# Attention values as the stationary operand, one-pass mask with minimum head by head, and normalized probabilities, in one layer of a hybrid GLA and windowed-attention backbone

## The chip, the cores and the metric

One core of a Trainium2 chip runs the whole kernel. The metric is device time in microseconds (us), from start to end of one execution. All figures below come from the measured times or from one profiled execution of the kernel before.

## The reference, cut to what matters

One layer on 512 latent tokens (four tiles of 128) and 128 context tokens (a fifth tile), D_MODEL 2048. The change touches only the windowed attention: 16 query heads of width 64 in four groups of four, each group sharing one key and value head. A latent tile reads its own and its neighbour key blocks, plus the cached context block; the context tile reads itself alone.

```
def sink_softmax(score_list, sink):
    s_sink = sink.astype(jnp.float32).reshape(SWA_KV_HEADS, SWA_GROUP, 1, 1)
    m = s_sink
    for sc in score_list:
        m = jnp.maximum(m, jnp.max(sc, axis=-1, keepdims=True))
    ps = [jnp.exp(sc - m) for sc in score_list]
    den = jnp.exp(s_sink - m)
    for p in ps:
        den = den + jnp.sum(p, axis=-1, keepdims=True)
    return [p / den for p in ps]
...
    p_ctx, p_band = sink_softmax([s_ctx, s_band], sink)
    o = jnp.einsum('bnhgqk,bkhd->bnqhgd', p_ctx, cvf) + jnp.einsum('bnhgqk,bnkhd->bnqhgd', p_band, vw)
```

Around it: modulated norm, one input projection (its last chunks are the queries), the gated linear attention, then two branch products with sigmoid gates ("the gate products"), an output product, a second norm, a router and 16 experts.

## The kernel before, in words

Every engine has its own instruction stream, written out by hand; semaphores join them. Large products run in "pieces" of 128 rows of weights: ScalarE rounds a piece's weights and tokens (the high halves, L458 and L459), VectorE subtracts them from the originals (the low halves, L462 and L465), TensorE makes three products for each token tile (L837). Four buffers of pieces (`spW`, `spX`) lie in memory that the attention stage uses for its own buffers. In the gate products VectorE also adds up a row of modulation for most pieces (L387, L390, in `mod_sums`).

The attention stage stands between the query projection and the gate products. It has 20 units: `units` orders them as tile 0 to 4 for key heads 0 and 1, then tile 0 to 4 for key heads 2 and 3, so that units 0 and 1 are tile 0, units 2 and 3 tile 1, and so on, and again from unit 10. A unit is four query heads of one tile against 3, 4, 4, 3 or 1 key blocks of 128 for tiles 0 to 4. Its steps:

- `scores(u)` on TensorE (L1110): four heads, each into its own PSUM bank (0 to 3). It waits for `sc_m`, the masks of the whole unit before, and signals `sc_pe` once.
- `softmax_front(u)` on VectorE: for each head one fused instruction scales, adds the mask and takes the maximum (L1932), then two small operations give the sink's difference and the negated maximum (L1938, L1939).
- `softmax_exps(u)` on ScalarE (L1544, L1547): waits for all of that, then the sink's exponential and four exponentials with their sums.
- `p_transposes(i)` on TensorE (L1138): four transposes of key block i into bank 4 or 5. Blocks 0 and 2 are copied out by ScalarE (L1564), blocks 1 and 3 by VectorE (L1956).
- `values(i)` on TensorE (L1148): for each of four heads one matmul, the transposed probabilities 128x128 stationary and 64 columns of values moving, output token by head width in bank 6.
- `o_rows(u)` on VectorE (L1963) multiplies by one over the sum; `o_transposes(u)` on TensorE (L1122) turns the result in bank 7, and `copy_o(u)` on ScalarE (L1553) puts it into `swT`, in the iteration after.
- `softmax_sums(u)` on VectorE (L1945, L1946): sum with the sink and reciprocal.

The loop over u issues, on TensorE: scores(u+2), transposes 0 and 1, then alternately a transpose and a value block; on ScalarE: copies of blocks 0 and 2 of u, copy_o(u-1), exponentials of u+2; on VectorE: copy of block 1, sums of u, masks of heads 0 and 1 of u+2, copy of block 3, masks of heads 2 and 3, o_rows(u). In the first four iterations VectorE also applies the rotary embedding to one of four remaining query tiles (`rope_q`, three operations of 512 columns), after a permutation on TensorE (`q_permuted`, L1079). Behind the loop ScalarE and VectorE prepare pieces 0 to 2 of the gate products, and those products begin.

## Time and profile before

| | |
|---|---|
| device time, median of 3 runs | 3020.17 us (3017.7 to 3020.69) |
| profiled execution | 3019.33 us, its span 3017.1 us, mean granted clock 0.978 |
| TensorE matmul busy | 2866.1 us (95% of the span) |
| VectorE busy | 2060.9 us (68%) |
| ScalarE busy | 1598.1 us (53%) |
| attention stage | 738.4 to 886.2 us from the span's start |

A share of busy time is an average over stages with different limits. What the change is worth is read from the attention stage alone: from the first score product (738.39) to the first matmul of the gate products (886.23). A matmul's record holds its latency too, and consecutive matmuls overlap, so their pace is read from the distance between starts.

### The profile page before, as it was taken

What the parts mean: (1) busy time and instruction counts of PE and PEld (TensorE: products, weight loads), DVE (VectorE), ACT (ScalarE), POOL (GpSimd) and SP (SyncE); (2) the same over time, 40 slices, a digit from 0 to 9 for tenths busy, and PEclk for the clock granted to TensorE, in tenths of its full rate; (3) what the DMA queues carried; (4) which work ended last, traced back from release to release, by engine and by line L of the source; (5) the groups of instructions that cost most, each with busy time, mean ns of one, the idle gap of its engine ahead of it and who ended that gap; (6) DMA issues with size and microseconds to landing.
All of it is one profiled execution on the core that took longest, in us unless ns stands there. A gap on an engine that the chain in (4) does not pass through costs nothing.

```text
span 3017.1 us, 38938 instructions
## 1 busy us (share of the span) xinstructions
PE 2866.1 (95%) x14261; PEld 2145.1 (71%) x14261; DVE 2060.9 (68%) x2367; ACT 1598.1 (53%) x1919; POOL 281.5 (9%) x182
## 2 busy tenths in 40 slices
PE   6999889999989999999999987999999999999993
PEld 4798548898878888887888873666666666666662
DVE  2436664544666667767665555888888888888884
ACT  4245324443554444434433343777777777777773
POOL 0000010000000000000001001111112112211111
PEclk9999999999999999999999997999999999999996
DMA  9822342221014343343462269999999999999994
GB/s 372 285 70 70 131 167 73 84 65 57 1 31 135 116 156 127 113 147 123 143 244 89 70 235 367 401 404 392 387 390 378 382 387 389 384 383 390 387 389 170
DMA packets 160799, 685.04 MB, mean 227 GB/s; under 512 B 13940, under 2 KB 14020, under 8 KB 99004
## 3 DMA queue, kind: packets, MB, share of 16 engines
q1 hardware_dynamic: 147216, 613.45, 53.2%
q0 software_dynamic: 11408, 69.78, 7.3%
q8 instruction: 78, 1.28, 0.2%
q10 hardware_dynamic: 2064, 0.26, 0.1%
q14 instruction: 33, 0.27, 0.0%
HBM read 651.91 MB, written 31.60 MB: 227 GB/s over the span
## 4 chain that ended last, share of the span: by engine, by line
PE 91%; DVE 4%; ACT 2%; DMA 2%; issue 1%; POOL 0%; DVEq 0%; POOLq 0%; ACTq 0%; SPq 0%
PE ps L837 38%; PE ps L1312 23%; PE ps L1339 12%; PE ps L856 5%; PE ps L863 3%; PE ps L1148 1%; PE ps L1285 1%; PE ps L1110 1%; PE ps L801 1%; DMA ring<-w_mod 1%; PE ps L1138 1%; ACT ar L1547 1%; PE ps L1006 1%; PE ps L1249 1%; PE ps L971 1%
## 5 line engine op out<-in xcount | busy, mean ns | idle before, releaser
L837 PE MATMUL ps<-split_weights,split_tokens 128*128 128x512 f32 x5040 | 1159.3, 391 | 8.1 <-issue 3.8
L837 PEld LDWEIGHTS ps<-split_weights,split_tokens 128*128 128x128 f32 x5040 | 944.8, 188 | 216.6 <-issue 16.7
L1312 PE MATMUL ps<-split_experts,split_xsT 128*80 128x512 f32 x3072 | 709.7, 392 | 4.8 <-DVE split_experts L2097 4.8
L1312 PEld LDWEIGHTS ps<-split_experts,split_xsT 128*80 128x80 f32 x3072 | 455.1, 148 | 257.6 <-DVE split_experts L2097 5.8
L462 DVE TENSOR_TENSOR split_weights<-ring,split_weights 128x512 fp32r<-128x512 f32 x384 | 267.8, 697 | 536.7 <-ACT split_tokens L459 534.8
L458 ACT ACTIVATE split_weights<-ring 128x512 fp32r<-128x512 f32 x384 | 242.7, 632 | 734.8 <-PE ps L837 612.3
L2097 DVE TENSOR_TENSOR split_experts<-hT,split_experts 128x2048 fp32r<-128x2048 f32 x240 | 548.0, 2289 | 77.2 <-ACT split_experts L1659 77.1
L1659 ACT ACTIVATE split_experts<-hT 128x2048 fp32r<-128x2048 f32 x240 | 460.7, 1920 | 153.6 <-PE ps L1312 114.4
L1339 PE MATMUL ps<-split_experts,split_hidT 128*80 128x512 f32 x1536 | 361.0, 394 | 0.0
L1339 PEld LDWEIGHTS ps<-split_experts,split_hidT 128*80 128x80 f32 x1536 | 225.5, 148 | 121.9
L465 DVE TENSOR_TENSOR split_tokens<-hT,split_tokens 128x640 fp32r<-128x640 f32 x304 | 249.4, 820 | 0.0
L2097 DVE TENSOR_TENSOR split_experts<-ring,split_experts 128x2048 fp32r<-128x2048 f32 x96 | 218.5, 2289 | 22.5 <-ACT split_experts L1659 22.5
L459 ACT ACTIVATE split_tokens<-hT 128x640 fp32r<-128x640 f32 x304 | 219.8, 723 | 0.0
L1659 ACT ACTIVATE split_experts<-ring 128x2048 fp32r<-128x2048 f32 x96 | 184.0, 1917 | 60.8 <-PE ps L1312 33.9
L856 PE MATMUL ps<-split_tokens,split_weights 128*128 128x384 f32 x768 | 185.8, 351 | 9.2 <-DVE split_tokens L489 9.2
L390 DVE SCALAR_TENSOR_TENSOR cst<-ring,cond,cst 128x512 f32<-128x512 f32 x240 | 169.1, 746 | 0.0
L856 PEld LDWEIGHTS ps<-split_tokens,split_weights 128*128 128x128 f32 x768 | 129.0, 194 | 24.1 <-DVE split_tokens L489 12.6
L863 PE MATMUL ps<-split_tokens,split_weights 128*128 128x256 f32 x768 | 136.5, 288 | 3.0 <-ACT ar L1520 1.8
L737 POOL DMA_INDIRECT y_rows<-ar,sidx x16 | 108.3, 6766 | 267.4 <-DVE ar L2125 267.4
L2097 DVE TENSOR_TENSOR split_experts<-ar,split_experts 128x2048 fp32r<-128x2048 f32 x48 | 109.7, 2286 | 28.6 <-ACT split_experts L1659 28.6
L863 PEld LDWEIGHTS ps<-split_tokens,split_weights 128*128 128x128 f32 x768 | 126.3, 193 | 4.0 <-ACT ar L1520 2.1
L1659 ACT ACTIVATE split_experts<-ar 128x2048 fp32r<-128x2048 f32 x48 | 91.9, 1915 | 21.5 <-PE ps L1312 13.0
(264 smaller groups left out, 1997.3 us busy)
## 6 DMA issues: line engine op xcount, KB each, us to landing
ring<-w_mod SPq DMA_DIRECT2D x96, 1024.0 KB, 5.3
hT<-w_exp_gate SPq DMA_DIRECT2D x80, 1024.0 KB, 7.2
hT<-w_exp_up SPq DMA_DIRECT2D x80, 1024.0 KB, 7.1
hT<-w_exp_down SPq DMA_DIRECT2D x80, 1024.0 KB, 9.3
ring<-w_in SPq DMA_DIRECT2D x64, 1024.0 KB, 5.3
ring<-w_exp_gate SPq DMA_DIRECT2D x32, 1024.0 KB, 8.0
ring<-w_exp_up SPq DMA_DIRECT2D x32, 1024.0 KB, 10.2
ring<-w_exp_down SPq DMA_DIRECT2D x32, 1024.0 KB, 7.5
```

The costliest lines, as they stand in the source:

```text
L390: dve.scalar_tensor_tensor(acc, v, c, acc, ALU.mult, ALU.add).then_inc(z_rd, 1)
L458: self.eng.activation(spW[:, s, 0, :], raw, ACT.Copy)
L459: self.eng.activation(spX[:, s, 0, :], (src[k] if type(src) is dict else src[:, k, :]), ACT.Copy).then_inc(piece_high, 1)
L462: a = self.eng.tensor_tensor(spW[:, s, 1, :], raw, spW[:, s, 0, :].bitcast(F32), ALU.subtract)
L465: self.eng.tensor_tensor(spX[:, s, 1, :], (src[k] if type(src) is dict else src[:, k, :]), spX[:, s, 0, :].bitcast(F32), ALU.subtract).the ...
L837: mm = pe.matmul(ps[:, b, :], spX[:, s, x, b * P:(b + 1) * P], spW[:, s, w, :], start=(k == 0 and x == w), stop=(k == n_k - 1 and x == 1))
L856: mm = pe.matmul(ps[:, c, 0:TA], spW[:, s, w, c * P:(c + 1) * P], spX[:, s, x, 0:TA], start=(k == 0 and x == w), stop=(k == KT - 1 and w = ...
L863: mm = pe.matmul(ps[:, 4 + c // 2, (c % 2) * TB:(c % 2 + 1) * TB], spW[:, s, w, c * P:(c + 1) * P], spX[:, s, x, TA:TOK], start=(k == 0 an ...
L1312: mm = pe.matmul(ps[0:CAP, bank + i, :], xsT[:, x, k, :], spE[:, s, w, col:col + BANK], start=(k == 0 and x == w), stop=(k == KT - 1 and x ...
L1339: mm = pe.matmul(ps[0:CAP, 4 + n, :], hidT[:, x, k, :], spE[:, s, w, n * BANK:(n + 1) * BANK], start=(k == 0 and x == w), stop=(k == FT - ...
L1659: act.activation(spE[:, s, 0, :], exp_slot[j % ESLOTS], ACT.Copy).then_inc(piece_high, 1)
L2097: dve.tensor_tensor(spE[:, s, 1, :], exp_slot[j % ESLOTS], spE[:, s, 0, :].bitcast(F32), ALU.subtract)\
```

## The change

The values become the stationary operand: two matmuls for each key block instead of four, each with 64 columns of values stationary and 256 columns of transposed probabilities (two heads) moving. Their output is already transposed, so that `o_rows`, `o_transposes` and their buffer go, and `copy_o(u)` reads bank 6 in the same iteration. The division by the sum moves ahead of the transposes: four multiplications of the probabilities in memory for each unit (`softmax_back`). The fused mask operation works on negated scores with a minimum, so that the negation of the maximum goes; it signals for each head, and scores and exponentials wait head by head. VectorE copies block 1 alone, between the masks of head 1 and head 2 of unit u+2; ScalarE copies blocks 0, 2 and 3. `q_permuted` stands ahead of the value products. The last two units have buffers of their own, and pieces 0 to 2 of the gate products are prepared during them.

```
-        orow = area(26112, 2, GRP * HD)
+        last_S = [area(27264 + BANK * i, BANK) for i in range(2)]
+        last_pT = [area(26112 + BANK * i, BANK) for i in range(2)]
-        copied_by = [(pt_cd if i % 2 else pt_cp) for t, _ in units for i, _ in enumerate(unit_keys(t)[1])]
+        n_units = len(units)
+        def S_of(u):
+
+            if u >= n_units - 2:
+                return last_S[u % 2].rearrange("p (j n) -> p j n", j=GRP)
+            return Sbuf[u % 3].rearrange("p (j n) -> p j n", j=GRP)
+
+        def pT_of(u, i):
+            return last_pT[u % 2] if u >= n_units - 2 else pT[:, u % 2, i * BANK:(i + 1) * BANK]
+
+        copied_by = [(pt_cd if i == 1 else pt_cp) for t, _ in units for i, _ in enumerate(unit_keys(t)[1])]
+        def copy_pT(act, u):
+
+            for i, _ in enumerate(unit_keys(units[u][0])[1]):
+                if i != 1:
+                    n = first_block[u] + i
+                    act.wait_ge(pt_pe, n + 1)
+                    if 2 <= u < n_units - 2:
+                        act.wait_ge(pv_pe, u - 1)
+                    act.activation(pT_of(u, i), ps[:, 4 + n % 2, :], ACT.Copy).then_inc(pt_cp, 1)
+
+        def copy_o(act, u):
+            t, g = units[u]
+            act.wait_ge(pv_pe, u + 1)
+            act.activation(swT[:, 2 * g:2 * g + 2, t * P:(t + 1) * P],
+                           ps[:, 6, 0:2 * P].rearrange("p (c q) -> p c q", c=2), ACT.Copy).then_inc(pv_cp, 1)
@@ -1099,28 +1124,18 @@
             def scores(u):
                 t, g = units[u]
-                if u:
-                    pe.wait_ge(sc_m, u)
                 for j in range(GRP):
+                    if u:
+                        pe.wait_ge(sc_mx, (u - 1) * (GRP + 1) + j + 1)
-                mm.then_inc(sc_pe, 1)
-
-            def o_transposes(u):
-
-                pe.wait_ge(pv_cp, u + 1)
-                pe.wait_ge(sq_rp, min(4 + u + 1, 8))
-                if u:
-                    pe.wait_ge(k_cp, 2 * SKV + u)
-                for c in range(2):
-                    mm = pe.transpose(ps[:, 7, c * P:(c + 1) * P], orow[:, u % 2, c * P:(c + 1) * P], ident)
-                mm.then_inc(k_tr, 1)
+                    mm.then_inc(sc_pe, 1)
@@ -1131,12 +1146,12 @@
-                        pe.wait_ge(sc_e, u + 1)
+                        pe.wait_ge(sc_n, u + 1)
-                                          Sbuf[u % 3][:, j * BANK + i * P:j * BANK + (i + 1) * P], ident)
+                                          S_of(u)[:, j, i * P:(i + 1) * P], ident)
-                    for j in range(GRP):
-                        mm = pe.matmul(ps[:, 6, j * HD:(j + 1) * HD],
-                                       pT[:, u % 2, i * BANK + j * P:i * BANK + (j + 1) * P],
-                                       svr[:, blocks[i], g * HD:(g + 1) * HD],
+                    for half in range(2):
+                        lo = half * HD
+                        mm = pe.matmul(ps[lo:lo + HD, 6, 0:2 * P], svr[:, blocks[i], g * HD:(g + 1) * HD],
+                                       pT_of(u, i).rearrange(
+                                           "p (c e q) -> p c e q", c=2, e=2)[:, :, half, :],
                                        start=(i == 0), stop=(i == len(blocks) - 1), skip_group_check=True)
+                if u < 4:
+                    q_permuted(4 + u)
+                else:
+                    if u == 4:
+                        pe.wait_ge(sq_rp, 8)
                 for i in range(len(blocks)):
                     if i + 2 < len(blocks):
                         p_transposes(i + 2)
                     values(i)
-                    if i == 0 and u:
-                        o_transposes(u - 1)
-                if u < 4:
-                    if u:
-                        pe.wait_ge(k_cp, 2 * SKV + u)
-                    q_permuted(4 + u)
-
-            o_transposes(len(units) - 1)
-            pe.wait_ge(k_cp, 2 * SKV + len(units))
+
+            pe.wait_ge(pv_cp, len(units))
             def softmax_exps(u):
-                act.wait_ge(sc_mx, u + 1)
                 sf = soft[:, u % 2]
-                act.activation(sf[:, 3, :], sf[:, 3, :], ACT.Exp)
                 for j in range(GRP):
-                    s = Sbuf[u % 3][:, j * BANK:j * BANK + len(blocks) * P]
-                    a = act.activation(s, s, ACT.Exp, bias=sf[:, 1, j:j + 1], accum_out=sf[:, 2, j:j + 1])
-                a.then_inc(sc_e, 1)
-
-            def copy_o(u):
-                t, g = units[u]
-                act.wait_ge(k_tr, SKV + u + 1)
-                act.activation(swT[:, 2 * g:2 * g + 2, t * P:(t + 1) * P],
-                               ps[:, 7, 0:2 * P].rearrange("p (c q) -> p c q", c=2), ACT.Copy).then_inc(k_cp, 1)
+                    act.wait_ge(sc_mx, u * (GRP + 1) + j + 1)
+                    s = S_of(u)[:, j, 0:len(blocks) * P]
+                    act.activation(s, s, ACT.Exp, bias=sf[:, 0, j:j + 1], scale=-1.0, accum_out=sf[:, 2, j:j + 1])
+                act.wait_ge(sc_mx, (u + 1) * (GRP + 1))
+                act.activation(sf[:, 3, :], sf[:, 3, :], ACT.Exp).then_inc(sc_e, 1)
 
             softmax_exps(0)
             softmax_exps(1)
             for u in range(len(units)):
-                for i in range(0, len(unit_keys(units[u][0])[1]), 2):
-                    act.wait_ge(pt_pe, first_block[u] + i + 1)
-                    if u >= 2:
-                        act.wait_ge(pv_pe, u - 1)
-                    to, src = pT_place(u, i)
-                    act.activation(to, src, ACT.Copy).then_inc(pt_cp, 1)
-                if u:
-                    copy_o(u - 1)
+                if u == n_units - 2:
+                    act.wait_ge(pv_pe, n_units - 2)
+                    gate_split(sp, 0, 0, 0, 1)
+                if u == n_units - 1:
+                    gate_split(sp, 0, 0, 1, AHEAD)
+                copy_pT(act, u)
                 if u + 2 < len(units):
                     softmax_exps(u + 2)
-            copy_o(len(units) - 1)
+                copy_o(act, u)
-            gate_split(sp, 0, 0, 0, AHEAD)
-            def softmax_front(u, heads):
-                dve.wait_ge(sc_pe, u + 1)
-                if u >= 3:
+                if 3 <= u < n_units - 2:
                 lo = {0: C_SW + P, 3: C_SW3, 4: C_SW + P}.get(t, C_SW)
                 for j in heads:
-                    a = dve.tensor_tensor_reduce(S[:, j, :], ps[:, j, 0:nk], cst[:, lo:lo + nk], HD ** -0.5,
-                                                 sink[:, GRP * g + j:GRP * g + j + 1], ALU.add, ALU.max,
-                                                 sf[:, 0, j:j + 1])
-                if GRP - 1 in heads:
-                    a.then_inc(sc_m, 1)
-                    dve.wait_ge(sc_m, u + 1)
-                    dve.tensor_tensor(sf[:, 3, :], sink[:, GRP * g:GRP * g + GRP], sf[:, 0, :], ALU.subtract)
-                    dve.tensor_scalar(sf[:, 1, :], sf[:, 0, :], -1.0, None, ALU.mult).then_inc(sc_mx, 1)
-
-            def softmax_sums(u):
-
+                    dve.wait_ge(sc_pe, u * GRP + j + 1)
+                    dve.tensor_tensor_reduce(S_of(u)[:, j, 0:nk], ps[:, j, 0:nk], cst[:, lo:lo + nk], -HD ** -0.5,
+                                             sink[:, GRP * g + j:GRP * g + j + 1], ALU.add, ALU.min,
+                                             sf[:, 0, j:j + 1]).then_inc(sc_mx, 1)
+                if GRP - 1 not in heads:
+                    return
+                dve.wait_ge(sc_mx, u * (GRP + 1) + GRP)
+                dve.tensor_tensor(sf[:, 3, :], sf[:, 0, :], sink[:, GRP * g:GRP * g + GRP], ALU.subtract).then_inc(sc_mx, 1)
+
+            def softmax_back(u):
                 sf = soft[:, u % 2]
                 dve.wait_ge(sc_e, u + 1)
                 ch.step(dve.tensor_tensor(sf[:, 2, :], sf[:, 2, :], sf[:, 3, :], ALU.add))
                 ch.step(dve.reciprocal(sf[:, 4, :], sf[:, 2, :]))
-
-            def copy_pT(u, i):
-
...
-            def o_rows(u):
-
-                dve.wait_ge(pv_pe, u + 1)
-                if u >= 2:
-                    dve.wait_ge(k_tr, SKV + u - 1)
-                dve.tensor_tensor(orow[:, u % 2, :].rearrange("p (j d) -> p j d", j=GRP),
-                                  ps[:, 6, 0:2 * P].rearrange("p (j d) -> p j d", j=GRP),
-                                  soft[:, u % 2, 4, :].unsqueeze(2).to_broadcast([P, GRP, HD]), ALU.mult).then_inc(pv_cp, 1)
-            softmax_front(0, range(GRP))
-            softmax_front(1, range(GRP))
+                for j in range(GRP):
+                    s = S_of(u)[:, j, 0:nk]
+                    a = dve.tensor_scalar(s, s, sf[:, 4, j:j + 1], None, ALU.mult)
+                a.then_inc(sc_n, 1)
+
+            ch.step(dve.tensor_scalar(sink[:, :], sink[:, :], -1.0, None, ALU.mult))
+            softmax_front(0)
+            softmax_front(1)
             for u in range(len(units)):
-                copy_pT(u, 1)
-                softmax_sums(u)
+                softmax_back(u)
                 if u + 2 < len(units):
                     softmax_front(u + 2, range(0, 2))
-                copy_pT(u, 3)
+                if len(unit_keys(units[u][0])[1]) > 1:
+                    n = first_block[u] + 1
+                    dve.wait_ge(pt_pe, n + 1)
+                    if u >= 2:
+                        dve.wait_ge(pv_pe, u - 1)
+                    dve.tensor_copy(pT_of(u, 1), ps[:, 4 + n % 2, :]).then_inc(pt_cd, 1)
                 if u + 2 < len(units):
                     softmax_front(u + 2, range(2, GRP))
-                o_rows(u)
                 if u < 4:
                     rope_q(4 + u)
-
+                if u == n_units - 2:
+                    dve.memset(mod_ones, 1.0).then_inc(z_rd, 1)
+                    gate_split(sp, 0, 0, 0, 1)
+
+            gate_split(sp, 0, 0, 1, AHEAD)
```

## Rows read from the trace of the kernel before

**Rows 1.** Busy time by stretch: us, then busy us (instructions) by engine, PEclk, DMA share

```profile
738.40:784.90 46.50, 40.90 (x295) 33.76 (x295) 31.49 (x90) 24.07 (x65) 0.00 (x0) 0.89 0.00 1
784.90:877.10 92.20, 84.42 (x735) 77.08 (x735) 53.88 (x201) 53.97 (x166) 0.00 (x0) 1.00 0.01 1
877.10:886.20 9.10, 3.83 (x30) 2.97 (x29) 3.34 (x11) 5.49 (x15) 1.17 (x1) 0.99 0.10 16
2000.00:2200.00 200.00, 200.00 (x912) 131.35 (x911) 175.56 (x95) 150.14 (x95) 38.23 (x12) 1.00 0.99 388
```

**Rows 2.** Timeline of TensorE, one iteration (u = 13): start us, us, what

```profile
841.67 2.11 PE L1110 MATMUL ps<-ar 64*128 64x384 f32 x16
843.70 1.09 PE L1138 MATMUL ps<-cst,ar 128*128 128x128 f32 x8
845.05 0.66 PE L1138 MATMUL ps<-cst,ar 128*128 128x128 f32 x4 [0.25 <-ACT ar L1564]
845.54 1.00 PE L1148 MATMUL ps<-ar 128*128 128x64 f32 x8
846.38 0.39 PE L1122 MATMUL ps<-cst,ar 128*128 128x128 f32 x2
846.60 0.60 PE L1138 MATMUL ps<-cst,ar 128*128 128x128 f32 x4
847.04 2.79 PE L1148 MATMUL ps<-ar 128*128 128x64 f32 x24
849.76 1.68 PE L1110 MATMUL ps<-ar 64*128 64x256 f32 x16
```

**Rows 3.** Timeline of TensorE in the linear attention, 64 stationary and 256 moving columns

```profile
405.21 1.95 PE L1006 MATMUL ps<-ar 128*64 128x256 f32 x16
...
418.64 0.65 PE L1006 MATMUL ps<-ar 128*64 128x256 f32 x4
```

**Rows 4.** Groups of VectorE by form, 600 to 900 us: busy us, mean ns | idle

```profile
L1932 DVE CUSTOM_DVE_ANT_0 ar<-ps,cst,sink 128x512 f32<-128x512 f32 x32 | 22.4, 747 | 0.3
L1932 DVE CUSTOM_DVE_ANT_0 ar<-ps,cst,sink 128x384 f32<-128x384 f32 x32 | 18.1, 615 | 19.3 <-PE ps L1110 19.1
L1956 DVE COPY ar<-ps 128x512 f32<-128x512 f32 x24 | 16.6, 692 | 34.2 <-PE ps L1138 34.2
...
L387 DVE TENSOR_SCALAR cst<-ring,cond 128x512 f32<-128x512 f32 x2 | 0.9, 482 | 0.0
```

**Rows 5.** Groups of ScalarE by form, 600 to 900 us

```profile
L1564 ACT ACTIVATE ar<-ps 128x512 f32<-128x512 f32 x36 | 21.3, 592 | 19.5 <-PE ps L1138 19.1
...
L1553 ACT ACTIVATE ar<-ps 128x256 f32<-128x256 f32 x20 | 7.7, 384 | 13.5 <-PE ps L1122 13.5
```

**Rows 6.** Chain that ended last: start us, us; four heads' exponentials, 512 and 128 columns

```profile
757.59 2.82 ACT ar L1547 x8
...
875.97 1.64 ACT ar L1547 x8
```

**Rows 7.** Timeline of the stage's start: first scores, second scores, third, first transposes

```profile
738.39 1.68 PE L1110 MATMUL ps<-ar 64*128 64x256 f32 x16 [1.14 <-ACT ar L1537]
742.40 2.88 PE L1110 MATMUL ps<-ar 64*128 64x256 f32 x16 [2.33 <-DVE soft L1932]
747.61 3.95 PE L1110 MATMUL ps<-ar 64*128 64x384 f32 x16 [2.33 <-DVE soft L1932]
751.49 2.46 PE L1138 MATMUL ps<-cst,ar 128*128 128x128 f32 x12
```

**Rows 8.** Busy time and granted clock (PEclk) by microsecond, the stretches at half clock

```profile
743.00:744.00 1.00, 1.00 (x9) 0.93 (x8) 0.00 (x0) 1.00 (x5) 0.00 (x0) 0.50 0.05 16
...
888.00:889.00 1.00, 1.00 (x4) 0.74 (x3) 1.00 (x3) 0.06 (x1) 0.00 (x0) 0.50 0.00 0
```

**Rows 9.** Timeline of a unit of tile 3 and of the stage's end, all engines

```profile
804.66 0.71 PE L1110 MATMUL ps<-ar 64*128 64x128 f32 x8
...
875.14 1.90 PE L1148 MATMUL ps<-ar 128*128 128x64 f32 x16
...
883.37 0.62 ACT L458 ACTIVATE split_weights<-ring 128x512 fp32r<-128x512 f32 x1
...
884.52 0.62 ACT L458 ACTIVATE split_weights<-ring 128x512 fp32r<-128x512 f32 x1
...
885.26 0.82 DVE L465 TENSOR_TENSOR split_tokens<-hT,split_tokens 128x640 fp32r<-128x640 f32 x1
...
886.23 14.00 PE L837 MATMUL ps<-split_weights,split_tokens 128*128 128x512 f32 x54 [3.17 <-DVE split_tokens L465]
```

More of the change, by code:

```diff
@@ L340, in build @@
         sq_pm, sq_rp, kv_ld = sem("rope_permuted"), sem("roped"), sem("cache_loaded")
-        k_dup, k_tr, k_cp, k_pm, k_rp, kv_st = (sem("k_doubled"), sem("k_then_o_transposed"), sem("k_then_o_copied"),
+        k_dup, k_tr, k_cp, k_pm, k_rp, kv_st = (sem("k_doubled"), sem("k_transposed"), sem("k_copied"),
                                                 sem("k_permuted"), sem("k_roped"), sem("cache_stored"))
-        sc_pe, sc_m, sc_mx, sc_e, pt_cd = sem("scores"), sem("scores_masked"), sem("scores_max"), sem("probs_exp"), sem("pT_copied_by_vector")
-        pt_pe, pt_cp, pv_pe, pv_cp = sem("p_transposed"), sem("pT_copied"), sem("pv_product"), sem("o_rows_normalized")
+        sc_pe, sc_mx, sc_e, sc_n, pt_cd = sem("scores"), sem("scores_masked_and_max"), sem("probs_exp"), sem("probs"), sem("pT_copied_by_vector")
+        pt_pe, pt_cp, pv_pe, pv_cp = sem("p_transposed"), sem("pT_copied"), sem("pv_product"), sem("pv_copied")
         gt_pe, gt_act, gt_dve = sem("gate_products"), sem("gate_sigmoid"), sem("gate_merged")
@@ L416, in build @@
         first_block = [sum(len(unit_keys(units[v][0])[1]) for v in range(u)) for u in range(len(units) + 1)]
-        copied_by = [(pt_cd if i % 2 else pt_cp) for t, _ in units for i, _ in enumerate(unit_keys(t)[1])]
+        n_units = len(units)
[6 more added lines that the diff above has]
+        copied_by = [(pt_cd if i == 1 else pt_cp) for t, _ in units for i, _ in enumerate(unit_keys(t)[1])]
         def pT_copied(pe, n):
             pe.wait_ge(copied_by[n], sum(c is copied_by[n] for c in copied_by[:n + 1]))
-        def pT_place(u, i):
-            return pT[:, u % 2, i * BANK:(i + 1) * BANK], ps[:, 4 + (first_block[u] + i) % 2, :]
+        def copy_pT(act, u):
[11 more added lines that the diff above has]
+                           ps[:, 6, 0:2 * P].rearrange("p (c q) -> p c q", c=2), ACT.Copy).then_inc(pv_cp, 1)
         def parts(*places):
@@ L1918, in _, with softmax_front @@
                     rope_q((k - 7) // 2)
-            def softmax_front(u, heads):
+            def softmax_front(u, heads=range(GRP)):
                 t, g = units[u]
-                _, blocks = unit_keys(t)
-                nk = len(blocks) * P
-                S = Sbuf[u % 3].rearrange("p (j n) -> p j n", j=GRP)[:, :, 0:nk]
+                nk = len(unit_keys(t)[1]) * P
                 sf = soft[:, u % 2]
-                dve.wait_ge(sc_pe, u + 1)
-                if u >= 3:
+                if 3 <= u < n_units - 2:
                     dve.wait_ge(pt_pe, first_block[u - 2])
@@ L1931, in softmax_front @@
                 for j in heads:
-                    a = dve.tensor_tensor_reduce(S[:, j, :], ps[:, j, 0:nk], cst[:, lo:lo + nk], HD ** -0.5,
-                                                 sink[:, GRP * g + j:GRP * g + j + 1], ALU.add, ALU.max,
-                                                 sf[:, 0, j:j + 1])
-                if GRP - 1 in heads:
-                    a.then_inc(sc_m, 1)
-                    dve.wait_ge(sc_m, u + 1)
-                    dve.tensor_tensor(sf[:, 3, :], sink[:, GRP * g:GRP * g + GRP], sf[:, 0, :], ALU.subtract)
-                    dve.tensor_scalar(sf[:, 1, :], sf[:, 0, :], -1.0, None, ALU.mult).then_inc(sc_mx, 1)
-            def softmax_sums(u):
+                    dve.wait_ge(sc_pe, u * GRP + j + 1)
[7 more added lines that the diff above has]
+            def softmax_back(u):
+                t, g = units[u]
+                nk = len(unit_keys(t)[1]) * P
                 sf = soft[:, u % 2]
@@ L2003, in gates_dve @@
                     dve.tensor_tensor(mrow[:, b, :], mrow[:, b, :], mtmp[b], ALU.add).then_inc(gt_dve, 1)
-            dve.wait_ge(pv_pe, len(units))
-            dve.memset(mod_ones, 1.0).then_inc(z_rd, 1)
-            gate_split(sp, 0, 0, 0, AHEAD)
             with dve.Fori(0, 3) as n:
```

7 lines of the change are left out of this document (removed).

## The prediction

> **What bounds the kernel now.** I read the 40 slices of the page first, then the busy time by stretch, then the timeline of TensorE through the attention stage, then the waits and the chain there. Outside the stage nothing is edited except the place of three pieces' preparation, so only the stage counts. It falls into three stretches [rows 1]: 46.5 us from the first score product to the first transposes of unit 4, 92.2 us to the last value product of unit 17, 9.1 us to the first gate product; 147.8 us together. In the middle one TensorE is busy 84.4 of 92.2 us at full clock (2.4 GHz), VectorE and ScalarE 54 each: TensorE bounds it, and its own order fixes the length. One iteration shows how [rows 2]: from 841.67 scores take 2.03, transposes 0 and 1 and the wait for ScalarE's copy of block 0 take 1.35, transpose 2 0.49, value block 0 0.84, the output's transposes 0.22, transpose 3 0.44, three value blocks 2.72; 8.09 us. The start is different: scores, masks and scores take turns, so that TensorE idles 2.33 us twice [rows 7], and the granted clock then falls to 0.50, its 1.2 GHz level [rows 8]; scores that take 2.11 us later take 3.95 there [rows 2, 7].
>
> **Part 1, the value products.** Removed are four matmuls for each block (0.84 us, or 0.9 in the run of three) and two output transposes (0.22 us) for each unit [rows 2]. Added are two matmuls with 64 columns stationary and 256 moving, each two records. The linear attention runs this very shape, also alternating between output partitions 0 and 64: 16 records in 1.95 us with the last one's latency, 4 in 0.65 [rows 3]. So four records, a block, cost 0.47 to 0.65; I take 0.50, nearer to the long run, since the next block follows at once. Four blocks save about 1.5 us, plus 0.22.
> The same rows speak on a rule. Sixteen records of 256 columns in 1.95 us [rows 3] are 0.46 to 0.48 ns a column; the sixteen score records of 384 and 128 columns in 2.03 us [rows 2] are 0.50. The pace of a column is the same, so the two halves do not overlap here. The Trainium skill ("TensorE: Matmul & The Clock Gate", in the section on why this matters for your kernels) says that matmuls with few output columns in distinct column groups run concurrently. By that rule a block would cost about half; its result is a rival below.
>
> **Part 2, VectorE.** Removed for each unit: the negated maximum, the second copy and the row multiplication. Added: four multiplications of the probabilities. The nearest row is a multiplication by a per-partition scalar of 512 columns from memory to memory, 482 ns [rows 4], against 692 for the copy from PSUM of the same size [rows 4]; two of them take 0.9 us together, and consecutive VectorE records overlap by some 0.08, so the pace is 0.41 for 512 columns. From 615 to 747 ns for 384 and 512 columns of the mask [rows 4], a block of 128 costs 0.13 at full rate, so about 0.07 here at the rate that 482 suggests: 0.34 for 384, 0.2 for 128. Bounds: 0.41 and 0.65 (the copy's pace). One iteration of four blocks on VectorE is then: masks 4 x 0.67 = 2.7, small operations 0.2, one copy 0.65, sums and reciprocal 0.4, multiplications 1.65; 5.6 us, in the shadow of TensorE as long as TensorE needs more. Once at the stage's start sixteen sinks are negated while the last projection still runs: nothing, and 0.2 us if it did not.
>
> **Part 3, ScalarE.** It gains the copy of block 3 (592 ns), keeps copy_o (384 ns) [rows 5] and the exponentials: four heads take 2.82 us for 512 columns and 1.64 for 128 [rows 6], so 2.43 for 384; the sink's adds 0.2. copy_o(u) now stands behind the exponentials of u+2, and ahead of copy 0 of u+1. Behind this queue stands transpose 2 of the next unit on TensorE, and value block 0 waits for copy_o itself since bank 6 is one. An iteration of four blocks on ScalarE from the start of copy 0: 0.6, wait for transpose 2 0.75, copies 2 and 3 1.35 with the wait between, exponentials 3.05, copy_o 0.4: 6.15 us. That is almost TensorE's own time, and where it is more, TensorE waits.
>
> **Part 4, the start and the first four iterations.** Scores and exponentials now follow each mask. Times from 738.39: first mask at 0.5, eight masks of 384 columns at 0.54 (615 ns less the overlap) and small operations to 5.2; scores(1) and scores(2) run in between, head by head. Sums and multiplications of unit 0: 0.4 + 4 x 0.34, so first transposes at 7.0; before, at 13.1 [rows 7]. Then VectorE bounds, since the rotary embedding stands in its queue: each of the four iterations has four masks of 512 (2.9 with the small ones), a copy 0.65, three operations of 512 columns for the embedding (2.15 at the copy's 692 ns), and the sums and multiplications of u+1 (1.75 once, 2.05 three times). 4 x 5.7 + 1.75 + 6.15 = 30.7. TensorE needs 2.0 + 1.2 + 0.9 (the permutation, which now fills the wait for copy 0) + about 2.6, less than 7.6. Unit 4's transposes start at 7.0 + 30.7 = 37.7, before at 46.5: 8.8 us gained.
>
> **Part 5, the middle.** From the first transpose of a unit to its last value product: 1.3 to transpose 2, 0.5 for it, 0.5 for value block 0, 0.44 for transpose 3, 3 x 0.48; 4.2 us for four blocks (six units: 25.2), 3.3 for three blocks (six units: 19.8), 1.8 and 2.0 for the two units of one block. Scores between them: 2.03 four times for four blocks [rows 2], 1.61 five times for three blocks (units 7, 10, 11, 16 and 17; 1.68 less the overlap) [rows 2], and 0.65 four times for one [rows 9]; 18.8 us. ScalarE's lateness, gone through unit by unit with Part 3's times: 1.05 for unit 6 and 1.1 for unit 16 (a short score product follows long exponentials), 0.55 for unit 14, and 0.1 to 0.2 five times; 3.45 us. Sum: 25.2 + 19.8 + 3.8 + 18.8 + 3.45 = 71.0 us against 92.2: 21.2 gained. VectorE finishes each unit's multiplications about 0.8 us before TensorE asks.
>
> **Part 6, the end.** Pieces 0 to 2 do not start before the last units, they start inside them and in ScalarE's queue: piece 0 waits for the values of unit 17 and stands ahead of unit 18's copy; pieces 1 and 2 stand ahead of unit 19's copy. A piece takes ScalarE 1.15 us (883.37 to 884.52) [rows 9]. From unit 17's last value: 1.2 + copy 0.65 + value 0.6 + copy_o 0.45 + two pieces 2.4 + copy 0.65 + value 0.6 + copy_o 0.45 + start 0.1 = 7.1 us, against 9.1 [rows 1]: 2.0 gained. VectorE's low halves and sums for piece 0 stand ahead of unit 19's multiplications, about 2.3 us, and end before ScalarE's pieces do. The preparation that stood exposed behind the stage (883.37 to 886.08) is covered by the two copies' waits only in part.
>
> **Sum.** Stage 37.7 + 71.0 + 7.1 = 115.8 against 147.8: 32 us. The profiled execution takes 3019.3 us (span 3017.1 and 2.2 around it), so 2987.3; it lies 0.8 under the median of 3020.17, which gives 2988. One cost has no row: three more waits for each score product. Its lower bound is zero, or a little less since they let scores start earlier; the upper is 0.1 us each, about 5 us in all. A satisfied wait between value blocks shows no gap in [rows 2], so I take it near zero, 1 us, and say 2989.
>
> **The rivals.**
> 1. VectorE bounds everywhere: if the multiplications run at 0.65, an iteration of four blocks takes 6.5 there, 0.2 above TensorE's, and each of the first four 0.9 longer: 5 us less gained, 2994. Against it speak 482 ns [rows 4].
> 2. The value products cost more: a strided moving operand could halve the rate, which gives 0.86 a block, as before. Then 50 blocks x 0.36 less what ScalarE's wait already holds, some 15 us less: 3004. No row has this stride; the shape itself is at full rate [rows 3].
> 3. The halves overlap: a block at 0.25. TensorE gets faster than ScalarE's 6.15, so only about 4 us come of it: 2985. [rows 3] speak against.
> 4. The gain is given back later. The experts run at a DMA share of 0.99 with 388 GB/s, and TensorE at 200 of 200 us [rows 1]. If the loads were bound to a time of their own, 3020 would stay. Against it: each load waits for a slot that TensorE and VectorE release, and the share before the experts is far lower (the page's slices), so the loads move with the rest.
> 5. Slower: the clock. With work cut by a fifth while VectorE and ScalarE set the pace, TensorE's idle parts could bring its clock down to 1.2 GHz again and again, as two idle times of 2.33 us did [rows 7, 8]. At that level an iteration of four blocks holds 5.8 us of work twice, about 12 us instead of 6.3. From six such iterations on (31 / 5.7) the gain is gone; with ten it ends at 2989 + 57 = 3046. Against it: the 7.8 idle us of the middle, in pieces, left the clock at 1.00 [rows 1], and the new pieces are by Part 5 mostly below 1.1 us.
>
> **How the numbers follow.** The forecast as worked out, with its unknowns, 2982 to 2998: 0.62. Rival 1: 0.09. Rival 2 in whole or part: 0.10. Rival 3: 0.08. Rival 4: 0.05. Rival 5: 0.06, of which a third ends still faster than before. The range of 2981 to 3003 holds the first, rivals 1 and 3 and a part of 2. 0.2% (6 us) is about what a measurement of this kernel can tell from no change. Faster by more: 0.91; within: 0.05; slower: 0.04.
>
> **What would show it.** First transposes of unit 0 near 7 us behind the first scores, and no score product of 2.9 or 3.95 us; value records four to a block at a pace of 0.12; multiplications at 0.48 for 512 columns; an iteration of four blocks at 6.2 to 6.4, TensorE idle before transpose 2 on ScalarE; last value of unit 17 at about 847, gate products at about 854. The prediction falls if the clock is at 0.50 in the middle, if value records stand 0.2 apart, or if TensorE waits for the multiplications in every unit.

## The result and the profile after

The changed kernel takes 2984.51 us (median of four, 2983.78 to 2985.76) against 3019.37 (median of four): ratio 0.9885, 95% interval 0.9868 to 0.9902, 34.9 us. The forecast was 2989, in a range of 2981 to 3003. The profiled execution took 2985.76 us, its span 2983.9, against 3019.33 and 3017.1.

The attention stage goes from 738.39 to 886.23 before, 147.8 us, and from 738.49 to 856.81 after, 118.3 us: 29.5 us. The two spans differ by 33.2 us; of the rest, 3.8 us lie behind the stage, where nothing is edited, and the repetition ("Changed again") returns to them. Busy time by stretch after, cut as [rows 1] is (us, then busy us and instructions of TensorE, its weight loads, VectorE, ScalarE, GpSimd; granted clock; DMA share; GB/s):

```profile
738.50:776.00 37.50, 32.16 (x232) 22.89 (x232) 35.60 (x101) 25.00 (x69) 0.00 (x0) 1.00 0.00 1
776.00:847.60 71.60, 65.82 (x528) 45.40 (x528) 61.92 (x221) 54.44 (x167) 0.00 (x0) 1.00 0.01 1
847.60:856.80 9.20, 3.55 (x16) 1.69 (x16) 7.22 (x19) 6.39 (x17) 0.16 (x1) 0.74 0.00 0
```

46.5, 92.2 and 9.1 us [rows 1] have become 37.5, 71.6 and 9.2. VectorE is busy 35.6 of the first 37.5 us: it bounds there. TensorE is busy 65.8 of the 71.6 us of the middle. The end has gained nothing, and its granted clock is 0.74 where it was 0.99.

The start, timeline of all engines (start us, us, what, idle before and who ended it), to be held against [rows 7]:

```profile
738.49 6.85 PE L1135 MATMUL ps<-ar 64*128 64x256 f32 x48 [1.14 <-ACT ar L1551]
739.56 0.62 DVE L1935 CUSTOM_DVE_ANT_0 ar<-ps,cst,sink 128x384 f32<-128x384 f32 x1 [13.55 <-PE ps L1135]
...
740.22 0.61 ACT L1560 ACTIVATE ar<-ar,soft 128x384 f32<-128x384 f32 x1 [0.49 <-DVE soft L1935]
...
744.67 1.41 DVE L1953 TENSOR_SCALAR ar<-ar,soft 128x384 f32<-128x384 f32 x4
...
746.13 1.09 PE L1153 MATMUL ps<-cst,ar 128*128 128x128 f32 x8 [0.80 <-DVE ar L1953]
```

The three score products run as one stretch beside the masks, the exponentials follow the first mask by 0.66 us, and the first transposes come 7.64 us behind the first scores instead of 13.1. The clock stays at 1.00 through the whole first stretch.

The same iteration as [rows 2] (u = 13), TensorE after:

```profile
820.03 2.11 PE L1135 MATMUL ps<-ar 64*128 64x384 f32 x16
822.06 1.09 PE L1153 MATMUL ps<-cst,ar 128*128 128x128 f32 x8
823.41 0.66 PE L1153 MATMUL ps<-cst,ar 128*128 128x128 f32 x4 [0.25 <-ACT ar L443]
823.99 0.65 PE L1164 MATMUL ps<-ar 128*64 128x256 f32 x4
824.58 0.66 PE L1153 MATMUL ps<-cst,ar 128*128 128x128 f32 x4
825.16 1.52 PE L1164 MATMUL ps<-ar 128*64 128x256 f32 x12
826.61 1.68 PE L1135 MATMUL ps<-ar 64*128 64x256 f32 x16
```

6.58 us instead of 8.09. The run of three value blocks takes 1.45 us from start to start where it took 2.72, the single block 0.59 instead of 0.84, and the output's transposes are gone. Costliest of the new groups, 700 to 870 us (busy us, mean ns, idle before):

```profile
L1164 PE MATMUL ps<-ar 128*64 128x256 f32 x240 | 32.6, 395 | 4.2 <-ACT ar L443 4.2
...
L1953 DVE TENSOR_SCALAR ar<-ar,soft 128x512 f32<-128x512 f32 x32 | 13.4, 482 | 0.3
...
L1953 DVE TENSOR_SCALAR ar<-ar,soft 128x384 f32<-128x384 f32 x32 | 11.3, 416 | 0.3
...
L1953 DVE TENSOR_SCALAR ar<-ar,soft 128x128 f32<-128x128 f32 x16 | 3.5, 283 | 0.1
```

The end, all engines:

```profile
846.08 1.52 PE L1164 MATMUL ps<-ar 128*64 128x256 f32 x12
...
848.31 0.36 ACT L448 ACTIVATE ar<-ps 128x256 f32<-128x256 f32 x1
...
848.58 0.62 ACT L483 ACTIVATE split_weights<-ring 128x512 fp32r<-128x512 f32 x1
...
849.72 0.58 ACT L443 ACTIVATE ar<-ps 128x512 f32<-128x512 f32 x1
849.85 0.69 DVE L487 TENSOR_TENSOR split_weights<-ring,split_weights 128x512 fp32r<-128x512 f32 x1 [1.91 <-ACT split_tokens L484]
...
850.45 0.65 PE L1164 MATMUL ps<-ar 128*64 128x256 f32 x4 [1.83 <-ACT ar L443]
...
851.41 0.62 ACT L483 ACTIVATE split_weights<-ring 128x512 fp32r<-128x512 f32 x1
...
852.39 0.88 DVE L1953 TENSOR_SCALAR ar<-ar,soft 128x128 f32<-128x128 f32 x4
...
853.08 0.73 ACT L484 ACTIVATE split_tokens<-hT 128x640 fp32r<-128x640 f32 x1
...
853.32 1.12 PE L1153 MATMUL ps<-cst,ar 128*128 128x128 f32 x4 [2.22 <-DVE ar L1953]
...
854.48 0.60 ACT L443 ACTIVATE ar<-ps 128x512 f32<-128x512 f32 x1 [0.67 <-PE ps L1153]
...
855.22 1.12 PE L1164 MATMUL ps<-ar 128*64 128x256 f32 x4 [0.78 <-ACT ar L443]
...
856.81 9.39 PE L862 MATMUL ps<-split_weights,split_tokens 128*128 128x512 f32 x36 [0.47 <-ACT ar L448]
```

VectorE stands still for 1.91 us waiting for ScalarE's half of piece 0, works on that piece from 849.85 to 852.0, and only then turns to unit 19's probabilities. TensorE waits 2.22 us for them, and within that wait, at 852, the clock falls to 0.50. ScalarE is ready for unit 19's copy at 853.81, when piece 2 ends, and waits 0.67 us for the transposes.

### The profile page after: what moved, and what is told of

Its sections match the earlier page's. It is cut to its first block, busy times and chain, and to the rows that moved or that the text cites. A ratio compares the mean times of both kernels' runs of the same rounds, so it can differ in the third digit from the quotient of the medians.

```text
span 2983.9 us, 38372 instructions
## 1 busy us (share of the span) xinstructions
PE 2838.4 (95%) x13981; PEld 2104.1 (71%) x13981; DVE 2072.6 (69%) x2400; ACT 1599.4 (54%) x1927; POOL 280.9 (9%) x182
## 4 chain that ended last, share of the span: by engine, by line
PE 91%; DVE 4%; ACT 2%; DMA 2%; issue 1%; POOL 0%; DVEq 0%; POOLq 0%; ACTq 0%; SPq 0%
PE ps L862 38%; PE ps L1326 24%; PE ps L1353 12%; PE ps L881 5%; PE ps L888 3%; PE ps L1299 1%; PE ps L826 1%; PE ps L1031 1%; PE ps L1153 1%; PE ps L1263 1%; PE ps L1164 1%; PE ps L1135 1%; PE ps L996 1%; DVE ar L1935 0%; DVE ar L1842 0%
```

## The experiments

Each starts from the changed kernel. Whole times turned out to spread more than most of the effects, in stretches that no kernel here edits, so each verdict goes by the stage in the run's profile: the first gate product's start less the first score product's start (both in us from the span's start). "Behind" is the span less the first gate product's start. Each stage is from one profile; the changed kernel has two, and they agree to 0.1 us. The medians come from four sessions, the last three of them on three different chips: the result; the four kernels from "waits by unit" on; the four from "pieces behind" on; the last two with "changed again". The kernel before took 3019.37, 3018.91, 3017.82 and 3018.68 us in them.

| kernel | median us | first scores at | first gate product at | stage us | behind us |
|---|---|---|---|---|---|
| before | 3019.37 | 738.39 | 886.23 | 147.8 | 2130.9 |
| changed | 2984.51 | 738.49 | 856.81 | 118.3 | 2127.1 |
| changed again | 2989.72 | 737.70 | 856.00 | 118.3 | 2129.3 |
| waits by unit | 2995.25 | 738.98 | 865.97 | 127.0 | 2128.4 |
| probabilities stationary | 3002.68 | 736.28 | 870.39 | 134.1 | 2129.8 |
| no multiplications | 2981.33 | 738.78 | 851.19 | 112.4 | 2128.2 |
| multiplications doubled | 3007.28 | 734.24 | 871.38 | 137.1 | 2130.4 |
| pieces behind | 2986.56 | 738.67 | 855.40 | 116.7 | 2130.1 |
| piece 0 only | 2985.07 | 735.32 | 850.79 | 115.5 | 2126.9 |
| copy 1 on ScalarE | 2985.18 | 741.52 | 857.43 | 115.9 | 2130.6 |
| the same, first four units | 2985.69 | 743.66 | 859.57 | 115.9 | 2131.1 |
| permutation behind | 2995.84 | 738.42 | 864.27 | 125.9 | 2128.9 |
| copies and end together | 2982.90 | 737.85 | 851.47 | 113.6 | 2128.2 |

**Waits by unit.**

```
-                for j in range(GRP):
-                    if u:
-                        pe.wait_ge(sc_mx, (u - 1) * (GRP + 1) + j + 1)
+                if u:
+                    pe.wait_ge(sc_mx, (u - 1) * (GRP + 1) + GRP)
+                for j in range(GRP):
...
-                    dve.wait_ge(sc_pe, u * GRP + j + 1)
+                dve.wait_ge(sc_pe, (u + 1) * GRP)
...
-                    act.wait_ge(sc_mx, u * (GRP + 1) + j + 1)
+                act.wait_ge(sc_mx, (u + 1) * (GRP + 1))
```

> The changed kernel, but scores, masks and exponentials wait for a whole unit again instead of head by head. My account: the first transposes come 3 to 4.5 us later than the changed kernel's 7.6 us behind the first scores, the granted clock may fall to its lower level there again, and the units of three blocks and of one block in the middle lose 2 to 4 us together, since ScalarE's exponentials start only after the last mask. Together 5 to 8 us slower than the changed kernel, 2990 to 2993 us. Rival, the gain lies in the cheaper value products and the rest is nothing: 2985 us within 1, first transposes still near 8 us.

Stage 8.7 us longer. TensorE's timeline at the start is that of [rows 7] again:

```profile
738.98 1.68 PE L1135 MATMUL ps<-ar 64*128 64x256 f32 x16 [1.14 <-ACT ar L1551]
743.11 2.87 PE L1135 MATMUL ps<-ar 64*128 64x256 f32 x16 [2.45 <-DVE soft L1934]
748.32 3.95 PE L1135 MATMUL ps<-ar 64*128 64x384 f32 x16 [2.33 <-DVE soft L1934]
752.20 1.76 PE L1153 MATMUL ps<-cst,ar 128*128 128x128 f32 x8
```

First transposes after 13.2 us, 5.6 later than changed, and the score products at 2.87 and 3.95 us again: the clock is at 0.50 from 744 to 753. That part was expected 1 us too small. Of the other 3.1 us, 0.6 lie in the first iteration, whose first transposes still run at half clock, and 2.4 in the middle, as expected. The head-by-head waits are worth 8.7 of the stage's 29.5 us.

**Probabilities stationary.** The output is left in another layout, so only its time counts.

```
-                    for half in range(2):
-                        lo = half * HD
-                        mm = pe.matmul(ps[lo:lo + HD, 6, 0:2 * P], svr[:, blocks[i], g * HD:(g + 1) * HD],
...
+                    for j in range(GRP):
+                        mm = pe.matmul(ps[:, 6, j * HD:(j + 1) * HD], pT_of(u, i)[:, j * P:(j + 1) * P],
+                                       svr[:, blocks[i], g * HD:(g + 1) * HD],
```

> The changed kernel, but each block has the old four value matmuls with probabilities stationary and 64 columns moving; the output is left in the order token by head width, without the transposes that would turn it, so the attention output is laid out wrongly and only the time counts. My account: a block costs 0.84 to 0.88 us instead of 0.48 to 0.58, 0.33 us more in 46 blocks outside the first four units; ScalarE's waits and VectorE's bound in the first four iterations hide part. 11 to 16 us slower than the changed kernel, 2996 to 3001 us. Rival, ScalarE or VectorE sets the pace and the value products are hidden: at most 3 us slower.

Stage 15.8 us longer, at the upper end. The same place of iteration 13, TensorE:

```profile
823.75 1.00 PE L1163 MATMUL ps<-ar 128*128 128x64 f32 x8
824.59 0.61 PE L1153 MATMUL ps<-cst,ar 128*128 128x128 f32 x4
825.04 2.79 PE L1163 MATMUL ps<-ar 128*128 128x64 f32 x24
```

0.84 and 2.72 us [rows 2], against 0.59 and 1.45. In the first four iterations, where VectorE bounds, the stage had lost 1.1 us by the first transposes of unit 4 (38.6 us behind the first scores against 37.5); 14.5 us more came in the middle. The value products are the largest part of the gain that an experiment shows, and TensorE does bound the middle. With the waits' 2.4 us they make 16.9 of the 20.6 us that the middle gained, if the two add; the output's transposes, 0.22 us for each of 14 units there before, would be 3.1 more, an estimate. No run puts back the transposes, the place of the division or the order of VectorE's queue by itself.

**No multiplications.** The division by the sum is left out.

```
-                for j in range(GRP):
-                    s = S_of(u)[:, j, 0:nk]
-                    a = dve.tensor_scalar(s, s, sf[:, 4, j:j + 1], None, ALU.mult)
-                a.then_inc(sc_n, 1)
+                dve.sem_inc(sc_n, 1)
```

> The changed kernel without the four multiplications of the probabilities by one over their sum, so the attention output is not normalized. My account, VectorE bounds the start and the first four iterations alone: TensorE's waits of 0.8, 1.40, 1.66, 0.49 and 0.92 us for it go, one more at the end, and the middle stays: 6 to 7 us faster than the changed kernel, about 2978 us. Rival, VectorE bounds every unit: 1.4 to 1.65 us of each, some 20 us, 2965 us. Other rival, TensorE or ScalarE bounds everywhere: nothing.

**Multiplications doubled.**

```
+                for j in range(GRP):
+                    s = S_of(u)[:, j, 0:nk]
+                    dve.tensor_scalar(s, s, 1.0, None, ALU.mult)
+                ch.step(dve.tensor_scalar(sf[:, 4, :], sf[:, 4, :], 1.0, None, ALU.mult))
```

> The changed kernel with the four multiplications done twice, the first time by 1.0 (and one small operation more). My account: VectorE gets 1.35 to 1.9 us more a unit, 8 to 9 us in the first part where it bounds already; in the middle its iteration of four blocks goes from 5.6 to 7.5 us and passes TensorE's 6.2, 12 to 14 us there: some 22 us slower than the changed kernel, 3007 us. Rival, VectorE is hidden in the middle even so: 9 us slower, 2994 us.

Stage 5.9 us shorter without (a little under the 6 to 7 expected; 5.2 of it before the end, 0.7 in the end), 18.8 us longer with twice as many. What TensorE waited for, changed kernel first, then doubled (waiting line, releaser, us in total, times, longest):

```profile
PE ps L1153 <- DVE ar L1953: 7.9, 7, 2.2
```

```profile
PE ps L1153 <- DVE ar L1957: 24.4, 19, 3.2
```

Seven waits, in units 0 to 4 and in the last two, become nineteen. So in the changed kernel TensorE waits for VectorE in the first part and at the end alone, and a second set of multiplications (1.4 to 1.7 us in a unit of three or four blocks) makes VectorE bound nearly everywhere. In the middle it has less than that to spare: unit 14's multiplications end 0.8 us before its transposes start. The rivals of 20 us and of nothing fall; the doubled one cost 3 us less than worked out, though two stretches of some 3 us at half clock are in it (from 745 and from 762).

**Pieces behind.** All three pieces behind the loop, as before (ScalarE and VectorE lose their calls of `gate_split` in the loop and get `gate_split(sp, 0, 0, 0, AHEAD)` behind it).

> The changed kernel, but pieces 0 to 2 of the gate products are prepared behind the attention loop again, on ScalarE and VectorE. The changed kernel needs 9.2 us from the last values of unit 17 to the first gate product. My account: inside the loop the pieces delay the last two units by as much as they save, since VectorE does piece 0 ahead of unit 19's multiplications and ScalarE pieces 1 and 2 ahead of its copy; behind it the first gate product comes after 7.5 us, 1.7 us earlier, so 1 to 2 us faster than the changed kernel. Rival, the prediction's own step: prepared inside the loop they gain 2 us, so 2 us slower here.

**Piece 0 only.**

```
-                if u == n_units - 1:
-                    gate_split(sp, 0, 0, 1, AHEAD)
...
+            gate_split(sp, 0, 0, 1, AHEAD)
             gates_act(0, True, False)
...
-                if u == n_units - 2:
-                    dve.memset(mod_ones, 1.0).then_inc(z_rd, 1)
-                    gate_split(sp, 0, 0, 0, 1)
...
-            gate_split(sp, 0, 0, 1, AHEAD)
+            dve.memset(mod_ones, 1.0).then_inc(z_rd, 1)
+            gate_split(sp, 0, 0, 0, AHEAD)
```

> The changed kernel, but only ScalarE's half of piece 0 stays inside the loop; VectorE does its half of piece 0 behind unit 19's multiplications, and pieces 1 and 2 come behind the loop on both. My account: VectorE's order is what holds unit 19, so the first gate product comes about 6 us behind the last values of unit 17 instead of 9.2, 3 us faster than the changed kernel, 2981 to 2982 us. Rival, ScalarE's pieces are the delay and VectorE's order is not: about 1.5 us faster, no more than with all pieces behind the loop.

Stage 116.7 and 115.5 against 118.3. From the last values of unit 17 (109.1 us behind the first scores in all three) to the first gate product: 9.2 us changed, 7.6 with the pieces behind, 6.4 with piece 0 alone in the loop. Preparing three pieces in the loop costs 1.6 us against not doing so; ScalarE's half of piece 0 there, with VectorE's half moved back, gains 1.2. "Piece 0 only" moves two things against the changed kernel, VectorE's half of piece 0 and ScalarE's pieces 1 and 2, so its 2.9 us don't show that VectorE's order alone held unit 19. The kernel without multiplications speaks against that: its unit 19 is ready earlier, ScalarE copies it right behind piece 2, and the end is only 0.7 us shorter. The whole medians (2986.56 and 2985.07) can't show this.

**Copy 1 on ScalarE**, in all units and in the first four.

```
+        def by_vector(u, i):
+            return i == 1 and False
...
-                if i != 1:
+                if not by_vector(u, i):
```

(in the second kernel `i == 1 and u >= 4`)

> The changed kernel, but ScalarE copies block 1 too, in all units. Theory A, ScalarE has 0.75 us free between its copies of block 0 and block 2 and the copy of block 1 fits there, while VectorE gets 0.65 us back where it bounds: 2 to 3 us faster than the changed kernel, all of it in the first four iterations. Theory B, the prediction's sum by which ScalarE needs 6.15 us in an iteration of four blocks, as much as TensorE: one more copy costs 0.6 us in ten to fourteen units, so 4 to 6 us slower than the changed kernel in spite of the gain in the first four.

> The changed kernel, but ScalarE copies block 1 in the first four units only, where VectorE bounds. 0.65 us for each of four iterations in both theories, 2 to 3 us faster than the changed kernel; if VectorE does not bound there, nothing, and if ScalarE does, slower.

Both stages 115.9 us, 2.4 shorter, and the first transposes of unit 4 at 35.1 in both. Theory A holds: all 2.4 us lie before unit 4, and the twelve copies more that the first of the two kernels puts on ScalarE behind it cost nothing. Its timeline in a middle unit of the kernel that copies all blocks there:

```profile
829.57 1.07 ACT L447 ACTIVATE ar<-ps 128x512 f32<-128x512 f32 x2
...
830.20 0.66 PE L1157 MATMUL ps<-cst,ar 128*128 128x128 f32 x4 [0.26 <-ACT ar L447]
```

The copy of block 1 follows that of block 0 at once, and TensorE's transpose 2 waits 0.26 us, as in the changed kernel.

**Permutation behind.**

```
-                if u < 4:
-                    q_permuted(4 + u)
...
                     values(i)
+                if u < 4:
+                    q_permuted(4 + u)
```

> The changed kernel, but the permutation of the next query tile stands behind the value products of each of the first four units again, instead of ahead of them. My account: VectorE's rotary embedding waits for it, and VectorE bounds there, so each of the four iterations gets 0.7 to 1.5 us longer: 3 to 6 us more in the stage. Rival, TensorE has slack and the place does not matter: the stage within 0.5 us of 118.3.

Stage 7.5 us longer, more than the account allowed. VectorE waits for the permutation in each of the four iterations (0.58, 0.58, 3.22 and 1.74 us, 6.1 in all), and behind two of TensorE's idle times the clock fell. Timeline of TensorE, and the clock in the microsecond 764 to 765:

```profile
761.96 1.09 PE L1153 MATMUL ps<-cst,ar 128*128 128x128 f32 x8 [1.54 <-DVE ar L1952]
763.30 1.11 PE L1153 MATMUL ps<-cst,ar 128*128 128x128 f32 x4 [0.25 <-ACT ar L443]
764.35 1.12 PE L1164 MATMUL ps<-ar 128*64 128x256 f32 x4
765.40 1.12 PE L1153 MATMUL ps<-cst,ar 128*128 128x128 f32 x4
```

```profile
764.00:765.00 1.00, 1.00 (x6) 0.31 (x5) 1.00 (x3) 0.55 (x1) 0.00 (x0) 0.50 0.00 0
```

A block that takes 0.59 us takes 1.05. The clock was at 0.50 again from 784 to 787, behind an idle time of 1.96 us. The four iterations are 0.5, 0.6, 3.2 and 1.7 us longer and unit 4 behind them 1.5. From a unit's first transposes to the permutation TensorE has the same work in the third and the fourth iteration, but takes 6.02 us (761.96 to 767.98) with the clock's fall and 4.55 without. So 1.5 us of the third iteration and the 1.5 of unit 4 are the lower clock, 3.0 together, and the other 4.5 are the wait for the permutation, which is what the account allowed.

**The two better parts together.** Copies of block 1 on ScalarE, and the end of "piece 0 only".

> The changed kernel with the copies of block 1 on ScalarE in all units and with piece 0 alone inside the loop (VectorE's half behind unit 19's multiplications). The two edits touch different parts, so their gains in the stage (2.4 and 2.9 us) add: stage 113.0 us, and 5 us less than the changed kernel in the median if disturbances elsewhere even out. If both only remove the same wait, the stage is 115.4 us.

Stage 113.6 us, 4.7 shorter than changed and 34.2 shorter than before; 0.6 over the sum, at the end. There TensorE's last wait but one is 2.26 us instead of the 1.84 of "piece 0 only", and the clock is at 0.50 from 848 instead of in the course of 849: unit 19's transposes take 1.12 us, not 0.66. Its median of 2982.90 lies 6.8 us under the changed kernel in the same session (ratio to before 0.9881, 0.9865 to 0.9898, against 0.9908, 0.9891 to 0.9925), and the four times of each do not overlap. It is the lowest of the kernels that leave nothing out; but two medians of the changed kernel lie 5.2 us apart, so the whole times show the direction and not the size.

**Changed again.** Nothing edited.

> The changed kernel once more, nothing edited. In its first profile the attention stage (first scores to first gate product) took 118.3 us and what follows 2127.1 us, 3.8 us less than in the kernel before, though nothing is edited there. If the 3.8 us belong to the change, the part behind the stage is 2127 us again, within 1. If they are the spread between executions, it lies anywhere from 2126.9 to 2131.1 us, the values of the eight experiments so far, while the stage is 118.3 us within 0.2.

Stage 118.3 us again. Behind it 2129.3, neither 2127 nor 2131. The twelve profiles of the changed kernel and its variants, which differ behind the stage in no more than where pieces 1 and 2 are prepared, show 2126.9 to 2131.1 us, and before's 2130.9 lies inside. So the 3.8 us that the first pair of profiles shows there need no cause in the change, nor do the 5.2 us between the two medians of one kernel (2984.51 and 2989.72); with one profile of before, a difference of 1 or 2 us there can't be excluded. What is shown to belong to the change is 29.5 us in the stage; the medians of the repetition's session give 29.0.

## Why the prediction was right

The time, 2984.5 (and 2989.7), lies in the range, and the stage was forecast at 115.8 against 118.3. The mechanism held in the start and the middle, failed at the end, and errors of opposite sign helped the sum. The 2.5 us by which the stage was missed are less than the 5.2 us between the changed kernel's two medians, so the whole time alone can't tell which step was wrong. By its parts:

- **Part 1, value products: right in mechanism, slightly off in size.** 0.48 a block in a run, as the linear attention's rows gave, but 0.59 where a transpose follows, and transposes 2 and 3 take 0.58 each between value blocks instead of 0.5 and 0.44. A body of four blocks takes 4.55 us (822.06 to 826.61), not 4.2. The halves do not overlap (rival 3): four records in 0.48 us are 0.12 a record of 256 columns. By the rule of the Trainium skill weighed there ("TensorE: Matmul & The Clock Gate", why this matters for your kernels), that such matmuls in distinct column groups run concurrently, a block would have taken about half of that, an estimate; the trace of the changed kernel does not agree. The strided moving operand costs nothing (rival 2).
- **Part 2, VectorE: right.** 482, 416 and 283 ns; 13.4 us for 32 of 512 columns, a pace of 0.42. Rival 1 falls by this and by the waits: TensorE waits for the multiplications in seven units of twenty, in none from 5 to 17.
- **Part 3, ScalarE: the step failed.** It counted the 0.75 us between the copies of block 0 and 2 as taken and so made ScalarE TensorE's equal; the copies on ScalarE show it free, with a copy of 0.6 us fitting in, and it is busy 4.55 of the 6.16 us from unit 13's transposes to unit 14's. Of 3.45 us of lateness, two waits were there: transpose 2 comes 1.90 us behind transpose 0 instead of 1.35 in units 6 and 16, 1.1 us together. This error and that of Part 1 (six units by 0.35, the three-block ones by 0.1) nearly cancel: 71.6 us against 71.0. That closeness is luck.
- **Part 4, the start and first four iterations: right.** 37.5 against 37.7, by two errors of 0.6 and 0.8 us that cancel. The first mask comes at 1.07, not 0.5, and the first transposes at 7.64, not 7.0; the iterations take 7.3 and three times 7.5 instead of 7.5 and 7.75. The waits by unit, the missing multiplications and the copies confirm who bounds it.
- **Part 6, the end: wrong.** 9.2 us, not 7.1; 2.1 of the 2.5 us by which the stage was missed lie here, and three terms hold them. The sum started ScalarE's piece 0 at unit 17's last value (847.60); ScalarE still had unit 19's exponentials and unit 17's copy_o in its queue and began at 848.58, so unit 18's copy is 0.9 us late. The step that VectorE's halves of piece 0 "end before ScalarE's pieces do" and so cost nothing left out that unit 19's multiplications and transposes stand behind it: ScalarE's pieces end at 853.81 and its copy starts at 854.48, 0.7 us. And the clock, put nowhere in the sum, fell while TensorE waited, so that the last copy, value block, copy_o and start take 2.3 us instead of 1.8. The two pieces themselves take 2.4 us as forecast.
- **Three more waits for each score product** were put at 1 us, and no run shows the upper bound of 0.1 us each. Scores for 512 keys take 2.03 us before and after (841.67 to 843.70, 820.03 to 822.06): nothing.
- **Rival 4** (given back later) did not come, by the column "behind". **Rival 5** (the clock) did not come in the middle, but it came at the end, for 0.5 us. The permutation's place, worth 3.0 us of lower clock, suggests that it was nearer than the forecast's 0.06.

## What to carry to other kernels

Where a small product has few output columns, put the narrow operand in the stationary place and stream the wide one, and read the price from the same shape elsewhere in the trace. Before filling an engine's wait with work for the next stage, list what stands ahead of that work and behind it in the same queue, on every engine: an early piece ahead of the last unit's first step can move the whole chain. Judge an edit of a stage by the stage in the profile when unedited stretches spread by more than the effect.

## What the runs showed of the hardware that was not expected

- Unedited stretches spread from run to run: 734.2 to 743.7 us before the stage and 2126.9 to 2131.1 behind it in thirteen profiles, while the stage of the changed kernel repeats to 0.1 us (118.3 and 118.3).
- The clock can fall where VectorE paces TensorE, and the length of an idle time alone doesn't tell. Idle times of 1.40 and 1.66 us ahead of the transposes of units 1 and 2 left it at 1.00 in the changed kernel. With the permutation behind, 1.27, 1.54, 1.54 and 1.96 us ahead of units 1 to 4, it was at 0.50 for 3 to 4 us behind the second and the fourth, and not behind the third. With the multiplications doubled it fell behind 2.08 us (unit 0) and 3.21 us (unit 2) and not behind 2.47 us (unit 4). In the changed kernel's end it fell at 852, behind 1.83 us and within the next 2.22.
- A value block ahead of a transpose costs 0.59 us (823.99 to 824.58), 0.1 more than a value block in a run.
